# A two-layer streaming encoder on one core: the first gather no longer waits for the gate, and each expert's combination moves four units later in the next expert, with its parts spread out

## What is computed

```python
for l in range(2):
    h = modulate(rms_norm(x, norm_mix[l]), sh1, sc1)
    proj = h @ w_in[l]                      # four mixers on its slices
    y = concatenate([ya, yb, yc, yd]) @ w_out[l]
    x = x + g1 * y
    h = modulate(rms_norm(x, norm_ffn[l]), sh2, sc2)
    f = swiglu(h, ...) if l == 0 else moe_ffn(h, ...)
    x = x + g2 * f
return rms_norm(x, norm_final)

def moe_ffn(h, ...):                        # 8 experts, 2 chosen for each token
    top_v, top_i = top_k(h @ router_w + router_b, 2)
    combine = one_hot(top_i) weighted by softmax(top_v)
    for e in range(8):
        y = y + combine[:, e] * (silu(h @ w1[e]) * (h @ w3[e])) @ w2[e]
```

## Time and profile before

| | |
|---|---|
| median of three runs (lowest, highest) | 1685.55 us (1678.83, 1688.5) |
| profiled execution, its own time | 1685.1 us |
| its span, first to last instruction | 1683.0 us |
| mean granted TensorE clock | 0.962 of full speed |
| PE busy / DVE busy / ACT busy, of the span | 96% / 79% / 59% |
| expert part of the span | from about 654 us to the end |

### The profile page before, as it was taken

The page is one execution under the profiler, slowest core; times in us unless marked ns, Lnnn a source line. Parts: engine busy times, 40 slices in busy tenths (PEclk is TensorE's granted clock), DMA queues, the critical chain, the costliest instruction groups (busy, mean ns, idle before and its releaser), DMA issues.

```text
span 1683.0 us, 19877 instructions
## 1 busy us (share of the span) xinstructions
PE 1610.0 (96%) x7987; PEld 1329.4 (79%) x7987; DVE 1333.4 (79%) x1277; ACT 988.4 (59%) x902; POOL 39.1 (2%) x108
## 2 busy tenths in 40 slices
PE   5999889999989997999999999999999999999997
PEld 5699489999977955887887887887887887887885
DVE  5687858877756355879979989979979979979887
ACT  1432244433452424777777777777777777777775
POOL 5200010000000000000000000000000000000000
PEclk9986989999988788999999999999999999999999
DMA  9648466788832204999999999989989999989990
GB/s 356 220 150 294 162 218 251 281 306 310 306 135 100 100 1 167 362 339 358 349 338 360 349 337 361 349 333 367 348 333 368 344 333 368 344 335 368 343 362 27
DMA packets 157144, 481.07 MB, mean 286 GB/s; under 512 B 4218, under 2 KB 6438, under 8 KB 157046
## 3 DMA queue, kind: packets, MB, share of 16 engines
q1 hardware_dynamic: 155120, 475.02, 76.4%
q0 software_dynamic: 1392, 3.58, 0.6%
q10 hardware_dynamic: 534, 1.13, 0.2%
HBM read 478.66 MB, written 1.05 MB: 285 GB/s over the span
## 4 chain that ended last, share of the span: by engine, by line
PE 85%; DVE 7%; ACT 3%; issue 2%; DMA 1%; SPq 1%; POOL 1%; DVEq 0%; ACTq 0%; POOLq 0%
PE bank L1015 17%; PE bank L1016 17%; PE bank L1017 17%; PE bank L767 4%; PE bank L912 3%; PE bank L943 3%; PE bank L941 3%; PE bank L942 3%; PE bank L819 2%; DVE ring_low L1596 2%; PE bank L989 2%; PE bank L764 2%; PE bank L956 2%; PE bank L958 2%; PE bank L957 2%
## 5 line engine op out<-in xcount | busy, mean ns | idle before, releaser
L1596 DVE TENSOR_TENSOR ring_low<-ring,w_high 128x2048 fp32r<-128x2048 f32 x336 | 766.5, 2292 | 118.9 <-ACT w_high L1983 113.3
L1983 ACT ACTIVATE w_high<-ring 128x2048 fp32r<-128x2048 f32 x336 | 644.6, 1919 | 250.5 <-PE bank L1017 242.4
L1015 PE MATMUL bank<-w_high,x_high 128*128 128x512 f32 x896 | 357.1, 399 | 4.1 <-DVE ring_low L1596 3.4
L1017 PE MATMUL bank<-w_high,x_low 128*128 128x512 f32 x896 | 353.2, 394 | 0.0
L1016 PE MATMUL bank<-ring_low,x_high 128*128 128x512 f32 x896 | 352.7, 394 | 0.0
L1015 PEld LDWEIGHTS bank<-w_high,x_high 128*128 128x128 f32 x896 | 168.3, 188 | 45.5 <-DVE ring_low L1596 6.8
L1017 PEld LDWEIGHTS bank<-w_high,x_low 128*128 128x128 f32 x896 | 168.3, 188 | 39.6
L1016 PEld LDWEIGHTS bank<-ring_low,x_high 128*128 128x128 f32 x896 | 168.2, 188 | 37.4
L1015 PE MATMUL bank<-w_high,act_high 128*128 128x512 f32 x448 | 178.5, 398 | 0.2 <-DVE ring_low L1596 0.2
L1016 PE MATMUL bank<-ring_low,act_high 128*128 128x512 f32 x448 | 177.8, 397 | 0.0
L1017 PE MATMUL bank<-w_high,act_low 128*128 128x512 f32 x448 | 176.2, 393 | 0.0
(11 more groups left out here) (311 smaller groups left out, 1800.5 us busy)
## 6 DMA issues: line engine op xcount, KB each, us to landing
ring<-in_moe_w_dram SPq DMA_DIRECT2D x168, 2048.0 KB, 7.9
ring<-in_w_mod_dram SPq DMA_DIRECT2D x23, 2048.0 KB, 10.8
ring<-in_ffn_w_dram SPq DMA_DIRECT2D x21, 2048.0 KB, 11.8
ring<-in_w_in_dram SPq DMA_DIRECT2D x8, 2048.0 KB, 15.1
ring<-in_w_out_dram SPq DMA_DIRECT2D x4, 2048.0 KB, 14.4
ring<-in_w_mod_dram SPq DMA_DIRECT2D x2, 1024.0 KB, 15.9
ring<-in_w_in_dram SPq DMA_DIRECT2D x2, 1024.0 KB, 18.7
gate_row<-in_b_mod_dram POOLq DMA_DIRECT2D x4, 512.0 KB, 7.5
```

The costliest lines, as they stand in the source:

```text
L1015: mm(out_, x_h, w_h, start=first, stop=False)
L1017: return mm(out_, x_l, w_h, start=False, stop=last)
L1596: tt_(moe_low(u, m // 2)[:, c], moe_slot(u, m // 2)[:, c], w_high[:, m % HIGHS, :].bitcast(F32), ALU.subtract).then_inc(low_made, 1)
L1983: act(w_high[:, m % HIGHS, :], moe_slot(u, m // 2)[:, c], ACT.Copy).then_inc(high_made, 1)
```

## The change

Six edits:

1. PE's wait for the gate moves from the end of `routing` to a place behind the first gather.
2. The combination stands behind unit 7 on PE (before: behind unit 3).
3. The spread transposes, which reuse the matrix that the combination reads, move from behind unit 7 to the middle of the next product, behind unit 9. They wait for the sum over bank 7, which is now the first one. ACT's copy to `spread` stays where it was, behind its unit 10.
4. On DVE the gate products and low parts of the old expert are spread one by one: gate product of half 0 behind unit 2, low part of half 0 behind unit 3, half 1 behind units 4 and 5. On ACT the copies to `y_high` stand behind units 3 and 5. The four sums go behind units 10 (one), 11 (two) and 12 (one); the products of the activations go from units 10 and 11 to 9 and 10, the next dispatch matrix from unit 12 to 13. The order of the banks changes with it.
5. At the end the parts alternate by halves: gate product 0, low part 0, gate product 1, low part 1.
6. The register with the largest number of tokens is read earlier on three engines: on DVE and ACT ahead of the experts, on SP ahead of the third expert's first transfer. The branch stays at the end.

```diff
-COMBINE = ((0, 0, 6), (1, 0, 4), (0, 1, 7), (1, 1, 5))
+COMBINE = ((0, 0, 7), (1, 0, 4), (0, 1, 6), (1, 1, 5))
...
@@ sync: load_pass
+                    if q == 0 and c == 2 * NCH:
+                        eng.wait_ge(route_v.sem, route_v.at("most_i"))
+                        most_tokens.append(eng.value_load(most_i[0:1, 0:1], min_val=0, max_val=T))
...
@@ tensor: routing, experts
                 mark(ins.then_inc(route_t.sem, 1), route_t, "most")
-                eng.wait_ge(gate_v.sem, gate_v.at("g1", 2 * DEPTH - 1))
...
                 if q == 0:
+                    eng.wait_ge(gate_v.sem, gate_v.at("g1", 2 * DEPTH - 1))
                     for g in range(NE // PAIR):
...
@@ tensor: one_expert
-                def up(J, name, first):
+                def up(J, name, first, middle=None):
...
                     for half in range(n_j):
+                        if half and middle:
+                            middle()
...
+                def spread_turn():
+                    if not is_first(q, g, u):
+                        eng.wait_ge(sum_v.sem, sum_v.at("a00", old))
+                    for tt in range(TT):
+                        ins = nc.tensor.transpose(bank[7][:, tt * P:(tt + 1) * P], dispatch[:, u, tt, :], ident)
+                    mark(ins.then_inc(moe_t.sem, 1), moe_t, "spread")
+
                 up(0, "w1", 0)
                 if is_first(q, g, u):
                     eng.wait_ge(route_v.sem, route_v.at("most"))
-                else:
+                up(0, "w3", 2)
+                if not is_first(q, g, u):
                     combine(old)
-                up(0, "w3", 2)
-
+                eng.wait_ge(moe_a.sem, moe_a.at("s1", r))
+                up(1, "w1", 0, spread_turn)
                 if not is_first(q, g, u):
                     eng.wait_ge(sum_v.sem, sum_v.at("a01", old))
-                for tt in range(TT):
-                    ins = nc.tensor.transpose(bank[7][:, tt * P:(tt + 1) * P], dispatch[:, u, tt, :], ident)
-                mark(ins.then_inc(moe_t.sem, 1), moe_t, "spread")
-
-                eng.wait_ge(moe_a.sem, moe_a.at("s1", r))
-                up(1, "w1", 0)
                 turn(0)
                 eng.wait_ge(moe_a.sem, moe_a.at("spread", r))
                 turn(1)
...
@@ vector: two_experts
                     for m in range(UNITS):
-                        if m == 2 and not first:
-                            y_gates(old, q, r)
                         if not first or m >= HIGHS:
                             low(r, u, m)
...
+                        if m in (2, 4) and not first:
+                            y_gate((m - 2) // 2, old, q, r)
+                        if m in (3, 5) and not first:
+                            y_rest((m - 3) // 2, old)
+                        if m == 10 and not first:
+                            sums(old, old_weight, 0)
+                        if m == 11 and not first:
+                            sums(old, old_weight, 1, 2)
+                        if m == 12 and not first:
+                            sums(old, old_weight, 3)
+                        if m in (9, 10):
+                            product(m - 9)
+                        if m == 13:
...
@@ scalar: two_experts
                         if not first or m >= HIGHS:
                             high(q, g, u, m)
-                        if m == 2 and not first:
-                            y_highs(old)
+                        if m in (3, 5) and not first:
+                            y_first((m - 3) // 2, old)
                         if m in (6, 7):
                             gated(m - 6)
                         if m == 10:
                             eng.wait_ge(moe_t.sem, moe_t.at("spread", r))
...
```

More of the change, by code:

```diff
@@ L212 @@
     "comb_v":
-        ("yg0 yg1 yl0 yl1").split(),
+        ("yg0 yl0 yg1 yl1").split(),
     "comb_a":
@@ L573, in _ @@
             load_pass(0)
+            with_more = most_tokens[0] > SLOTS
             store(0)
-            eng.wait_ge(route_v.sem, route_v.at("most_i"))
-            with eng.If(eng.value_load(most_i[0:1, 0:1], min_val=0, max_val=T) > SLOTS):
+            with eng.If(with_more):
                 load_pass(1)
@@ L1597, in low, with y_gate, y_rest, sums @@
                     ALU.subtract).then_inc(low_made, 1)
[L1599 to L1618, removed]
+            def y_gate(half, rep, q, r):
+                if half == 0 and isinstance(r, int) and r == NE and q == 0:
+                    eng.wait_ge(half_t.sem, half_t.at("y"))
+                else:
+                    eng.wait_ge(unit_used, used_at(r, -1))
+                done(eng, tt_(act_m[:, half, :], bank[4 + half][:, :], gate_row[:, half * W:(half + 1) * W],
+                              ALU.mult).then_inc(comb_v.sem, 1), comb_v, f"yg{half}", rep)
+            def y_rest(half, rep):
+                c = slice(half * W, (half + 1) * W)
+                eng.wait_ge(comb_a.sem, comb_a.at(f"yh{half}", rep))
+                done(eng, tt_(y_low[:, c], act_m[:, half, :], y_high[:, c].bitcast(F32),
+                              ALU.subtract).then_inc(comb_v.sem, 1), comb_v, f"yl{half}", rep)
+            def sums(rep, weight, *which):
+                for tt, half, b in (COMBINE[n] for n in which):
                     eng.wait_ge(comb_t.sem, comb_t.at(f"c{tt}{half}", rep))
@@ L1695, in experts @@
                 end = combined(q, expert(q, 0, NE))
-                y_gates(end, q, expert(q, 0, NE))
-                y_lows(end)
-                sums(end, choice[:, 1, 2, :] if q else chosen[:, 2, NE - 1, :], slice(0, 4))
+                for half in range(2):
+                    y_gate(half, end, q, expert(q, 0, NE))
+                    y_rest(half, end)
+                sums(end, choice[:, 1, 2, :] if q else chosen[:, 2, NE - 1, :], 0, 1, 2, 3)
             def final(rep):
@@ L1776, in _ @@
             eng.wait_ge(s_final, 16)
+            with_more = eng.value_load(most_i[0:1, 0:1], min_val=0, max_val=T) > SLOTS
             experts(0)
             final(0)
-            with eng.If(eng.value_load(most_i[0:1, 0:1], min_val=0, max_val=T) > SLOTS):
+            with eng.If(with_more):
                 eng.wait_ge(s_out, 16 * STORES)
@@ L1983, in high, with y_first @@
                 act(w_high[:, m % HIGHS, :], moe_slot(u, m // 2)[:, c], ACT.Copy).then_inc(high_made, 1)
[L1985 to L1989, removed]
+            def y_first(half, rep):
+                eng.wait_ge(comb_v.sem, comb_v.at(f"yg{half}", rep))
+                done(eng, act(y_high[:, half * W:(half + 1) * W], act_m[:, half, :], ACT.Copy).then_inc(comb_a.sem, 1),
+                     comb_a, f"yh{half}", rep)
             def two_experts(q, g):
@@ L2063, in experts @@
                         two_experts(q, g)
-                y_highs(combined(q, expert(q, 0, NE)))
+                for half in range(2):
+                    y_first(half, combined(q, expert(q, 0, NE)))
             def final(rep):
```

4 lines of the change are left out of this document (2 added, 2 removed).

## The result

| | before | changed kernel |
|---|---|---|
| median of the first comparison, us | 1686.69 (1678.83 to 1688.5) | 1702.15 (1699.02 to 1705.31) |
| ratio of the first comparison | | 1.0100 [1.0078, 1.0122] |
| median of a second comparison, us | 1685.73 (1678.09 to 1688.78) | 1707.23 (1706.95 to 1710.76) |
| ratio of the second comparison | | 1.0139 [1.0114, 1.0165] |
| first profiled execution, us | 1685.1 | 1699.02 |

The forecast was 1702.7 us. The first comparison agrees with it to 0.6 us, the second is 4.5 us above. So the changed part of the program costs some 20 to 22 us rather than 17.6, and that the first median lies within 0.6 us of the forecast is partly luck.

A forecast was written before the change was run, and what follows sets the result against it. PE was taken to bound the kernel, busy 126.07 of 126.56 us per expert. The terms 17.8 + 8.3 - 5.2 - 2.5 - 0.8 = +17.6 us on 1685.1 gave 1702.7 us, range 1695 to 1709.

The forecast's parts named there:

- DVE's lag: DVE's queued work behind the stop at unit 11 makes PE wait again at units 12 to 15: 8.3 us.
- the clock: Full rate was expected inside the experts, so the sum held nothing for it; half rate there would prove the prediction wrong.
- The start: At the first gather: it begins 3.36 us earlier, part lost to the half-rate stretch; gain 2.5 us.
- The stop at the fourth unit: PE's 0.7 us stop at unit 3 goes in seven experts as DVE's parts are spread; gain 5.2 us.
- ACT's copy and the stop at unit 11: ACT's copy to `spread` waits for PE's later transposes, delaying `w_high`; PE stops 2.2 us in eight experts: 17.8 us.
- rival D: The stops also pull the clock down, once per expert, 41 us in all: 1744 us; 6%.
- End and registers: At the program's end: alternating by halves gives 0, at best 0.1 us; moving DVE's register load gains 0.8 us.

The follow-up runs named there:

- alone: Kernel before, with only the first gather ahead of the wait for the gate and the register read early on SP, DVE and ACT; 1681.62 us, ratio 0.9986.
- the smaller stop: Changed kernel with the spread transposes behind six of unit 9's twelve matmuls; 1691.96 us, ratio 1.0051.
- the first and third experiments: First: changed kernel with ACT's copy to `spread` behind unit 12, 1677.74 us; third: kernel before with only the spread transposes moved behind unit 9, 1711.78 us.

## Why the prediction came out right, step by step

The time, the sign, and the cause of the stop are as forecast. Two terms aren't: DVE's lag, priced at 8.3 us, cost nothing, and the clock, which the sum left out, cost 12.5. The forecast had named the sign of it: it was to be wrong "if the half rate shows up inside the experts", and it did. The size came out near all the same because two errors offset each other, which is luck.

**The start, -2.5.** Measured -2.9 and -3.5 in the changed kernel, -3.9 alone, of which the first expert takes back some 0.2. The mechanism is as told. I had left the half-rate stretch where it was; it changed its length between executions instead (3.4 us in one, about 7 in another, 10.2 before), and with it what the start gives.

**The stop at the fourth unit, -5.2.** Gone in every later run with the spread parts: 7 x 0.72 = 5.0.

**ACT's copy and the stop at unit 11, +17.8.** Right in place, chain and size: 8 x 2.3 = 18.4. The four hand-overs came within 0.07 us of the computed times.

**DVE's lag, +8.3: this step failed.** DVE was as late as forecast: ring_low of units 12 to 15 ended at 817.42, 820.41, 823.38 and 827.04, T + 8.9, 11.9, 14.9 and 18.5. But PE didn't need them when I had said. Unit 11 began at 813.70, and with the half rate in it and the eight transposes behind it unit 12 came at 818.94, 13 at 821.81, 14 at 824.59 and 15 at 827.37: all behind DVE. The term measured nothing: units 12 to 15 follow each other as in the kernel without any stop. At full rate unit 15 would have been due at 825.8, and the smaller stop showed such a lag at its forecast size.

**The clock, not in the sum: +12.5.** The forecast's sum put the clock at nothing. In place of DVE's term came eight half-rate stretches that cost 1.56 us each. This is the mechanism of rival D, which I gave 6% and priced at 5.1 us an expert from the long stretch ahead of the first gather; the true price was a third of it. The argument against it, that short single stops leave the clock alone, rested on a stop of 0.7 us; one of 2.3 us doesn't. The rule of the Trainium skill, "TensorE: Matmul & The Clock Gate" (section "HAM oscillation — how this bites in real kernels"), that an array which is made to wait falls back to the half rate again and again, agrees in kind with the granted clock of 0.51 behind the stop, though here 5 of 24 such stops, in three executions, brought no fall. I should have priced a middle case between none and 5.1 us.

**End and registers, 0 and -0.8.** 0 and -1.0. SP's wait for the last engine fell from 1.0 to 0.2 us; its wait for its own store grew from 1.7 to 2.6, since its own register load, at 1678.9 before, no longer stands ahead of that wait.

With the measured sizes the sum is 18.4 + 12.5 + 0.2 (the first expert's unit 7) - 5.0 - 2.9 - 1.0 = +22.2, as in the first trace. With seven half-rate stretches (10.9) and -3.5 at the start it is +20.0, as in the second. The medians of the second comparison are 21.5 apart. The forecast of +17.6 missed the trace by about 4.5 us: an error of -12.5 and one of +8.3 offset each other. The sign and the cause, one copy in ACT's order, are shown by the first and third experiments; that the lower clock hid the lag is worked out from DVE's and PE's rows and from the smaller stop, since no expert of the changed kernel with sums had the full stop at full rate. Open is why the same stop brought the half rate in eight, seven and four of eight experts.

## What to carry to other kernels

When an instruction is moved on one engine, move its consumer on every engine that works in order, or count what is queued behind that consumer: here a copy of 0.37 us, left two units too early, cost about 29 us. Slack has to be read at the unit where the wait will stand (1.0 us), not from busy shares (ACT 74%). And a stop in dense matmul work has two prices, its length and the half-rate stretch that may follow, and the second changes which later waits still show.

## What the runs showed of the hardware that I had not expected

A single stop of 2.3 us in otherwise dense work was followed by some 3.4 us at 1.2 GHz, in 8 of 8, 7 of 8 and 4 of 8 experts of three executions; stops of 0.9 us were followed by none in eight. In the first two executions the clock fell 0.9 to 1.0 us after the restart. In the third it fell within 0.5 us of the restart: in its fourth expert PE starts at 1086.64, and 1087.29 already takes 0.63 us. In each case PE's matmuls were 0.427 instead of 0.233 us apart.

The same register load differed by engine and place. On DVE it took 0.55 us at its new place, against 0.85 at the end of the program, on SP 0.47 against 0.71, and on ACT it stayed the same, 0.46 against 0.47. DVE's:

```profile
L1790 DVEq TENSOR_LOAD <-most_i x1: 545/545/545, 646.6 to 646.6; - x1
```

The part ahead of c, which no edit touched, differed by up to 11.6 us between executions, more than half of what was being measured.
